# The second layer's modulation weights consumed during the first layer's merge, one piece behind each output tile

## The reference, cut to what matters

```python
# x: 256 latent tokens, ctx: 256 context tokens, D = 1024, two layers; all float32
mod = silu(c) @ w_mod[l] + b_mod[l]          # w_mod: (2, 1024, 6144): shift, scale, gate, twice
h = rms_norm(x) * (1 + scale1) + shift1
p = h @ w_in[l]                              # q, k, v, pool, hyena, and 3 x 1024 gate columns
ys = [attention(p), pool(p), hyena(p)]       # 512 wide each
merged = sum(sigmoid(gate_n) * (ys[n] @ w_branch[l, n]))
x = x + gate1 * (merged @ w_out[l])
h2 = rms_norm(x) * (1 + scale2) + shift2
x = x + gate2 * moe(h2)                      # 16 experts, top 2
```

## Time and profile before

| | |
|---|---|
| three runs | 1735.78, 1738.56, 1742.26 us, median 1738.56 |
| profiled execution | 1740.76 us, its span 1739.0 us |
| PE busy | 1495.9 us, 86% of the span |
| DVE, ACT, POOL busy | 850.8, 635.6, 368.8 us |
| DMA | 374.32 MB, mean 215 GB/s |
| granted TensorE clock | mean 0.929 of full |

### The profile page before, as it was taken

How to read it: one execution, slowest core, us unless ns; L and a number is a source line. 1 busy time by engine, 2 the same in 40 slices (tenths; PEclk the granted TensorE clock), 3 DMA queues, 4 the chain that set the end, 5 groups by cost and what they waited for, 6 DMA issues and landing times. The chain is left out here.

```text
span 1739.0 us, 19624 instructions
## 1 busy us (share of the span) xinstructions
PE 1495.9 (86%) x7748; PEld 1076.0 (62%) x7748; DVE 850.8 (49%) x1204; ACT 635.6 (37%) x848; POOL 368.8 (21%) x206
## 2 busy tenths in 40 slices
PE   6998998789999977999999787679889986977772
PEld 2465677568788746788888535468679973322322
DVE  4621765762223246899999556144764633100002
ACT  2422222372232242778777434223164441000003
POOL 0223222112233301111010122335226631000001
PEclk8999999899999986999999888889899997999996
DMA  8457221102232315899999772752314657999992
GB/s 298 170 194 274 74 73 49 36 11 73 92 126 72 121 32 226 343 401 406 406 400 400 252 262 85 294 202 97 100 43 152 206 203 293 420 420 423 422 375 85
DMA packets 120003, 374.32 MB, mean 215 GB/s; under 512 B 8270, under 2 KB 74000, under 8 KB 88944
## 3 DMA queue, kind: packets, MB, share of 16 engines
q1 hardware_dynamic: 109168, 334.58, 51.0%
q0 software_dynamic: 10752, 38.61, 5.9%
HBM read 356.39 MB, written 16.78 MB: 215 GB/s over the span
## 5 line engine op out<-in xcount | busy, mean ns | idle before, releaser
L658 POOL TENSOR_TENSOR w_lo<-ring,w_hi 128x1024 fp32r<-128x1024 f32 x120 | 299.2, 2503 | 629.3 <-ACT w_hi L1431 629.2
L775 PE MATMUL bank<-h_hi,w_hi 128*128 128x512 f32 (+1 forms) x768 | 272.1, 354 | 15.5 <-DVE h_lo L1753 10.8
L776 PE MATMUL bank<-h_hi,w_lo 128*128 128x512 f32 (+1 forms) x768 | 265.2, 345 | 0.0
L777 PE MATMUL bank<-h_lo,w_hi 128*128 128x512 f32 (+1 forms) x768 | 264.7, 345 | 0.0
L775 PEld LDWEIGHTS bank<-h_hi,w_hi 128*128 128x128 f32 x768 | 148.6, 194 | 53.4 <-issue 27.4
L776 PEld LDWEIGHTS bank<-h_hi,w_lo 128*128 128x128 f32 x768 | 149.1, 194 | 16.8 <-issue 1.2
L777 PEld LDWEIGHTS bank<-h_lo,w_hi 128*128 128x128 f32 x768 | 148.7, 194 | 16.9
L775 PE MATMUL bank<-w_hi,h_hi 128*128 128x512 f32 (+1 forms) x384 | 142.5, 371 | 9.9 <-DVE w_lo L2058 5.1
L1431 ACT ACTIVATE w_hi<-ring 128x1024 fp32r<-128x1024 f32 x120 | 125.3, 1053 | 63.3 <-DMA ring<-in_w_in 34.2
L777 PE MATMUL bank<-w_lo,h_hi 128*128 128x512 f32 (+1 forms) x384 | 139.3, 363 | 0.0
L776 PE MATMUL bank<-w_hi,h_lo 128*128 128x512 f32 (+1 forms) x384 | 138.9, 362 | 0.0
(11 more groups left out here) (284 smaller groups left out, 2891.3 us busy)
## 6 DMA issues: line engine op xcount, KB each, us to landing
ring<-in_w_in SPq DMA_DIRECT2D x52, 1024.0 KB, 5.1
ring<-in_w_up_e SPq DMA_DIRECT2D x52, 1024.0 KB, 8.7
mix<-in_w_gate_e SPq DMA_DIRECT2D x51, 1024.0 KB, 8.2
ring<-in_w_mod SPq DMA_DIRECT2D x48, 1024.0 KB, 7.3
operands_plain<-in_w_down_e SPq DMA_DIRECT2D x29, 1024.0 KB, 25.8
mix<-in_w_down_e SPq DMA_DIRECT2D x20, 1024.0 KB, 8.0
ring<-in_w_down_e SPq DMA_DIRECT2D x15, 1024.0 KB, 7.1
y_rows<-mix POOLq DMA_DIRECT2D x24, 512.0 KB, 8.1
```

The source lines that it names most:

```text
L658: pool.tensor_tensor(w_lo[:, slot], rview(raw, 8)[:, :, x * P:(x + 1) * P], w_hi[:, slot].bitcast(F32), ALU.subtract).then_inc(w_l, 1)
L775: first = mm(dst, stat[0], mov[0], start=start, stop=False)
L776: mm(dst, stat[1], mov[0], start=False, stop=False)
L777: return first, mm(dst, stat[0], mov[1], start=False, stop=stop)
```

## The change

All 24 `w_mod` pieces of layer 1 leave the ring and the stages named above. They are loaded one at a time into `mod_next`, 2048 columns of `mix` beside the ring that attention has done with, and PE consumes one behind each of the 24 tiles of layer 0's merge. SP issues a piece when PE is done with the one before (`m_us`), at a fixed point of its list between the ring pieces. The results go to `mods_next`, since layer 0's `mods` are still needed. ACT copies each finished third (`mod_rows`), PE transposes it behind tile 2 of the next group (the last third behind tile 2 of the output projection) and DVE takes it. PE's loop over the groups is written out, in both layers. The router's weights `wrt`, which lay in the place that the pieces now use, are loaded by POOL after the last residual and no longer before attention, and PE waits for them ahead of the router's matmuls (L1119). Some small buffers move.

```diff
             for g in range(2 * IN_C - AHEAD):
                 if g % 2 == 0:
                     order.append(("in", l, (g + AHEAD) // 2))
-                if g in MOD_AFTER:
+                if l == 0 and g in MOD_AFTER:
                     order += [("mod", l, DK + 2 * MOD_AFTER[g] + h) for h in range(2)]
...
-            if l + 1 < DEPTH:
-                order += [("mod", l + 1, k) for k in range(DK)]
...
+            def mod_piece(p):
+                if p:
+                    sp.wait_ge(m_us, p)
+                else:
+                    sp.wait_ge(a_o[0], len(units_of[0]))
+                i, k = divmod(p, DK)
+                sp.dma_start(mod_next, a["w_mod"][1, k * P:(k + 1) * P, i * RW:(i + 1) * RW]).then_inc(s_lds, 16)
+
+            mod_behind = {at_of[("merge", 0, 0)] + 6 * n + i: [8 * n + k for k in ks] for n in range(3)
+                          for i, ks in ((2, (0,)), (3, (1, 2, 3)), (5, (4,)), (6, (5, 6, 7)))}
...
-                    if at == lo + RS:
+                    if at == lo + RS * (1 - l):
                         filter_transforms(l)
...
                     sp.dma_start(rview(at % RS, k), src).then_inc(ring_full[at % RS], 16)
+                    for p in mod_behind.get(at, []):
+                        mod_piece(p)
...
-                pool.dma_start(wrt, a["w_router"]).then_inc(r_ld[l], 16)
...
                 pool.wait_ge(o_d[l], 16 * l + 8 * streams(l))
+                pool.dma_start(wrt, a["w_router"]).then_inc(q_io[l], 16)
                 pool.dma_start(iota, a["iota"]).then_inc(q_io[l], 16)
...
             def mod(l, i, k):
...
+                if l:
+                    pe.wait_ge(s_lds, transforms_to(0) + 16 * (DK * i + k + 1))
+                    w = mod_next
...
-                last.then_inc(ring_used, 1)
+                last.then_inc(m_us if l else ring_used, 1)
...
-                with pe.Fori(0, 3) as n:
+                for n in range(3):
                     for m in range(DK):
...
+                        if l == 0:
+                            mod(1, n, m)
+                            if n and m == 2:
+                                mod_columns(1, n - 1)
                     pe.wait_ge(g_pe[l], n * (2 * DK) + (2 * DK))
                     pe.nop().then_inc(w_u, 1)
...
+                    if l == 0 and m == 2:
+                        mod_columns(1, 2)
...
+                pe.wait_ge(q_io[l], 32 * (l + 1))
                 for k in range(DK):
                     pe.wait_ge(n_h, (2 * l + 1) * DK + k + 1)
                     last = mm(bank[7][0:E_N, 0:T], wrt[:, k, :], hT[:, k, 0:T], start=k == 0, stop=k == DK - 1)
...
                     filter_in(l + 1, 0)
-                    mods_and_filters(l + 1, range(DK))
+                    filter_in(l + 1, 1)
+                    filters(l + 1, 0)
+                    spectra_a(l + 1, 0)
+                    spectra_b(l + 1, 0)
...
+                        if l == 0 and n and m == 0:
+                            mod_rows(1, n - 1)
...
+                        if l == 0 and n and m == 3:
+                            mod_take(1, n - 1)
```

More of the change, by code:

```diff
@@ L400, in build, with mod_of, transforms_to @@
         e_s = sem("output_stored")
+        def mod_of(l, i, n, s):
+            return mods[:, i:i + n, s] if l == 0 else mods_next[:, MOD_T * s + i:MOD_T * s + i + n]
+        def transforms_to(l):
+            return 16 * (4 + l * (2 + MOD_C))
         def mbank(i):
@@ L782, in mod_columns @@
                 for x in range(4):
-                    last = tp(mbank(i)[:, x * P:(x + 1) * P], mrow[:, i % 2, x * P:(x + 1) * P], ident)
+                    rows = mrow_next if l else mrow[:, i % 2]
+                    last = tp(mbank(i)[:, x * P:(x + 1) * P], rows[:, x * P:(x + 1) * P], ident)
                 last.then_inc(m_co[l], 1)
@@ L1381, in mod_rows @@
             def mod_rows(l, i):
+                if l:
+                    act.wait_ge(m_us, DK * (i + 1))
+                    if i:
+                        act.wait_ge(m_co[l], 3 * l + i)
+                    A(mrow_next, mbank(i)[:, :], ACT.Copy).then_inc(m_ev[l], 1)
+                    return
                 act.wait_ge(ring_used, direct_to[at_of[("mod", l, DK * i + DK - 1)]])
@@ L1757, in mod_take @@
                 dve.wait_ge(m_co[l], 3 * l + i + 1)
+                if l:
+                    for s in range(2 if i == 0 else 1):
+                        last = V.tensor_tensor(mod_of(l, 16 * i, 16, s).rearrange("p (c x) -> p x c", c=4),
+                                               mbank(i)[:, :].rearrange("p (x c y) -> p x c y", x=4, c=4)[:, :, :, s],
+                                               par[l][:, C_BMOD + 16 * i:C_BMOD + 16 * i + 16]
+                                               .rearrange("p (c x) -> p x c", c=4), ALU.add)
+                    last.then_inc(m_tk[l], 1)
+                    return
                 V.tensor_tensor(mods[:, 16 * i:16 * i + 16, :].rearrange("p (c x) s -> p x c s", c=4),
@@ L1763, in gains @@
             def gains(l, w):
-                for s in range(2):
-                    last = V.scalar_tensor_tensor(gs[:, w, :, s], mods[:, (3 * w + 1) * DK:(3 * w + 2) * DK, s], 1.0,
+                for s in range(2 if l == 0 or w == 0 else 1):
+                    last = V.scalar_tensor_tensor(gs[:, w, :, s], mod_of(l, (3 * w + 1) * DK, DK, s), 1.0,
                                                   par[l][:, C_G1 + 8 * w:C_G1 + 8 * w + 8], ALU.add, ALU.mult)
@@ L1861, in _ @@
                         gate_scales(l, 1)
-                    if g == 9:
+                    if l == 0 and g == 9:
                         mod_take(l, 1)
-                mod_take(l, 2)
+                if l == 0:
+                    mod_take(l, 2)
                 dve.wait_ge(m_tk[l], 3 * l + 3)
                 gains(l, 1)
-                V.tensor_scalar(half_gate[:], mods[:, 2 * DK:3 * DK, :], 0.5, None, ALU.mult).then_inc(m_d[l], 1)
+                for s in range(S):
+                    last = V.tensor_scalar(half_gate[:, :, s], mod_of(l, 2 * DK, DK, s), 0.5, None, ALU.mult)
+                last.then_inc(m_d[l], 1)
                 link(V.memset(up[:, :, 0:POOL_PAD], 0.0))
```

77 lines of the change are left out of this document (42 added, 35 removed).

## The result

The kernel after took 1712.81 us in the median of four runs (1710.84 to 1716.68), the kernel before 1737.17 beside it (1734.64 to 1742.26). The ratio is 0.985, with a 95% interval of 0.983 to 0.987: 24.4 us faster. The forecast was 1715.8 with a range of 1708 to 1731. In a later comparison of five rounds the unchanged kernel after stood at 0.987 (0.985 to 0.990).

The account below looks back on a forecast made before the run. TensorE, busy for 86% of the span, was taken to bound most stages, while layer 1's projection waited for DMA. Terms -45.4 - 1.5 + 23.1 + 1.0 = -22.8 us take the median from 1738.56 to 1715.8, range 1708 to 1731.

Parts of the forecast that it names:

- Layer 1's projection: End of tile 1 to the pooling products: without 16 pieces and two transposes, 105.6 us become 60.2, saving 45.4.
- its 18 us of waits: Layer 1's projection: the modulation's matmuls waited 18.0 us for their pieces, on a ring shared with projection weights.
- The transition: Between the layers: eight pieces and one transpose removed gain up to 4 us, the lower clock loses some 2.5: -1.5.
- The rows of 1004 to 1008 us: Transition before: clock granted at 0.50, L815 at 0.90 us a matmul; cited as agreeing that activity releases the throttle.
- The merge: Layer 0's merge, bounded by PE: 24 pieces and three transposes added cost 23.1 us, ends 21 and 26.
- The single place: Layer 0's merge: one place gives each piece some 9.2 us to land against a 7.6 median; lateness costed at nothing.
- Rival (b): Layer 0's merge: pieces land late, at 10.5 us or more, costing 31 us; 1747 us in all, chance 0.06.
- The loop: PE's loop written out: matmuls follow at the same spacing, costed at nothing, ends -1 and +3 us.
- The router: Router weights loaded later: one more POOL issue goes ahead and PE waits for both; +1 us, ends 0 and 2.
- (a): Layer 1's projection does not close up, through splits or clock: 32 us saved instead of 45, 1729 us, chance 0.15.
- (c): Layer 1's projection: waits only change their name, 22 us saved and eaten by the added 23; 1738 us, chance 0.09.
- The sum: Whole kernel: projection -45.4, transition -1.5, merge +23.1 and router +1.0 give -22.8 us.

Follow-up runs that it names:

- The experiment on this part alone: Kernel before without the 16 modulation pieces, copies and transposes in layer 1's projection, nothing computed in their place: 1700.91 against 1740.39 us, ratio 0.976.
- the second run: Kernel after, unchanged, run again beside the kernel before: 1718.60 us, ratio 0.987.
- the fillers: Kernel after with unread matmuls in the transition's waits, alone or also ahead of both routers (17 and 11, 8 and 5): 0.984, 0.986, 0.983 of the kernel before.
- the halves: Kernel after with each modulation piece loaded as two halves, the second issued when the first has landed: 1727.65 against 1739.20 us, ratio 0.994 to the kernel before.
- the experiment: Kernel before with TensorE's loop over the merge's three groups written out in both layers, nothing else: 1733.11 against 1740.39 us, ratio 0.9957.
- the quarters: Kernel after with each modulation piece loaded as four quarters, each issued when the one before has landed: 1813.19 us, ratio 1.041 to the kernel before.

## Why the prediction was right

**Layer 1's projection, -45.4 predicted.** -43.2 by the starts; with the last products' own duration the stretch is 62.0 us against the 60.2 that were worked out. The missing 1.8 us are mostly the 1.31 that the last L981 wait for DVE: the text had let the former 2.50 us go whole. The experiment on this part alone gave the same 43.7. What the prediction did not ask is what its 18 us of waits were made of: less than half go with the bytes, the rest with the ring's order, and the clock of 0.86 came on top. All three went with the pieces, so that the sum held.

**The transition, -1.5.** -2.2 to the first tile, and the mean over all traces is -2.3 to the experts' transposes. Its argument held: the two pieces on the chain are gone, and L856 starts at half clock and pays 1.5 us for it (3.1 in the second run). Over six traces without pieces this loss is 2.2 us in the mean, where 2.5 had been assumed. That the size came out so near is in part luck, as the loss runs from 1.4 to 3.1 us between traces. The rule of the Trainium skill that the prediction weighed, that activity releases the throttled clock (TensorE: Matmul & The Clock Gate, What's actually happening), is borne out in kind by the fillers: more activity gave the higher clock. The rows of 1004 to 1008 us, which the prediction calls agreement, are not: PE was busy for all four of those microseconds and the clock stayed at 0.50. Where the two differ the measurement decides, and busy time alone did not raise the clock there.

**The merge, +23.1.** +25.5, the term with the largest error, and inside the bounds of 21 to 26. The mechanism is right, the sizes are not, and that they come within 2.4 us is in part luck. Too low: a piece inside a group costs 1.19 us, not 1.01, which is 3.8 us over 21 pieces; the three at group ends cost 0.73 each and not 0.2, another 1.6, as the written-out loop leaves a wait of 0.30 us there and not 0.89, so that less was there to be filled. Too high: only two of the three transposes lie in the merge, 0.39 each (0.5 us less); the loop itself gave back 1.24. By the rows 21 x 1.19 + 3 x (1.65 - 0.69 - 0.23) + 2 x 0.39 = 28.0 us come out over the written-out loop, where 1.65 is the distance from the last matmul before a piece to the second one behind it (451.35 to 453.00), and 26.7 were measured; see the last section for 0.95 of the rest.

**The single place, at nothing.** Right in the outcome, but the room was mis-sized: 8.3 us and not 9.2, as a piece is issued when the one before is finished and wanted one tile later, and its own time is no part of that. So the cover at a landing of 7.6 us was 0.7 and not 1.6. It held since the pieces landed in 4.9 us, 5.8 at the most. With 7.7 in the median, as with the halves, five of 24 were late. Rival (b) is real with 11.0 us, and dearer than forecast: 92 us, where the prediction's 24 for each microsecond over 9.2 gives 43.

**The loop, at nothing.** By the experiment it was worth 2.3 us over both merges, outside the bound of -1. The rows at group ends had been read as the wait for the product alone; 0.2 to 0.6 us of it were the loop's.

**The router, +1.0.** The router of layer 1 started 1.06 us later behind the start of the output projection, and 0.61 of it is PE's wait, 5.97 us in place of 5.36; the other 0.45 are slower steps in the projection's tiles (last section). The wait is for iota, as expected:

```profile
1406.00 5.11 PE L1156 MATMUL bank<-mix 128*16 128x256 f32 x16 [5.97 <-DMA mix<-in_iota]
```

The delay hardly reached the end: from the start of that projection to PE's last group are 334.1 us before and 334.3 after. As a cost to the whole the term was too high.

**The rivals.** (a) and (c) are excluded by the stretch of 61 us at a clock of 1.00 with PE busy for 96% of it, (b) by a merge without a wait for DMA.

**The sum, -22.8.** -24.1 by the trace. The terms miss by 2.2 us (projection), -0.7 (transition), 2.4 (merge) and -2.7 (the two last rows of the table together, -1.7 in place of the router's +1.0), and the three rows without a term moved by -2.5. So the mechanism of each large term is shown, but that they add up to within 1.3 us is partly luck.

## What to carry to other kernels

Cut the trace into stages at the same instructions before and after: the stages of unchanged code then show how far runs differ by themselves, and a term of 2 us can be read where the median of runs can't tell it. Work that feeds on weights can be moved to a stage that PE bounds while its memory path has room; here its price was PE's time alone, some 20% more than its matmuls' duration for the steps around them, and only while each load lands well within its room. A rest of PE can cost twice, once as a wait and once as the lower clock of the work behind it (64 and 26 us with the quarters), so price a late load with the clock. A higher clock for a group of matmuls is worth nothing where something else ends the stage, as at layer 1's router. Take the room of a load from its issue to the start of its use, and look at what the removed work had kept warm.

## What the runs showed of the hardware

- A loop on PE around three groups cost 0.59, 0.47 and 0.23 us at its ends in layer 0, as far as the distance of two matmuls can show it, in one trace of each; in three other traces with the loop the first end was 0.1 us shorter.
- Steps between 512-column matmuls of the merge with nothing between them are 0.2287 us in the mean before and 0.2276 after (854 and 814 steps), 0.95 us over 864 steps. With three pieces left in place of 24 they are 0.2270. The two kernels differ so elsewhere too, and not always to the gain of the new one: 0.2333 and 0.2278 in the output projection of layer 0 (180 steps each), 0.1184 and 0.1203 between the 256-column matmuls of layer 1's merge (788 and 780), and 0.1178 and 0.1200 in its output projection (181 each). The loop written out alone leaves the first at 0.2287. No run here says why.
- Layer 1's merge can't be compared as a whole. With the loop written out it took 108.1 us in five of the kernels built on after and 109.6 in three, in which the clock over its first 10 us was 0.83 and not 1.00. The distances at the group ends are free of that.
- Busy is not always enough for the clock: in the kernel after, within 1022 to 1030 us, PE was busy for 7.19 of 8 us with matmuls of 64 rows, at a granted clock of 0.50 throughout. Behind it the same spectrum matmuls took 5.1 to 6.8 us in six traces without pieces, and 3.7 in three and 5.4 in one of the four with pieces.
- The same or nearly the same code up to the merge of layer 0 took from 372.2 to 381.7 us in thirteen traces; from the first tile of its projection to the last pooling product it took 136 to 141. That scatter alone is as large as most single terms of this change.
